# Page numbers read four or six at a time, ahead of the wait for the buffer

## The reference

```python
rows_c = pool_cmp[page_table].reshape(b, past_len, N_KV_HEADS, 2, HEAD_DIM)
o_c, imp = cmp_branch(q, compress(rows_c, w_cmp), q_pos, rel_bias, k_gain[0])
...
_, idx = lax.top_k(score, n_top)
phys = page_table[jnp.arange(b)[:, None, None, None], start // page]
rows = pool[phys[..., None], off, gi]
return sel_attend(q, rmsnorm(rows[..., 0, :], k_gain), rows[..., 1, :], k_pos, q_pos, rel_bias)
```

## Time and profile before

| | us |
|---|---|
| median of 3 runs | 1231.87 (1231.04 to 1232.95) |
| the profiled execution | 1229.76 |
| its span, first to last instruction | 1227.5 |
| PE busy | 1179.2 (96%) |
| DVE, ACT, POOL busy | 477.9, 286.2, 221.9 |

### The profile page before, as it was taken

The page is one execution under the profiler, slowest core; times in us unless marked ns, Lnnn a source line. Parts: engine busy times, 40 slices in busy tenths (PEclk is TensorE's granted clock), DMA queues, the critical chain, the costliest instruction groups (busy, mean ns, idle before and its releaser), DMA issues.

```text
span 1227.5 us, 36608 instructions
## 1 busy us (share of the span) xinstructions
PE 1179.2 (96%) x14724; PEld 971.6 (79%) x14724; DVE 477.9 (39%) x1383; ACT 286.2 (23%) x763; POOL 221.9 (18%) x376
## 2 busy tenths in 40 slices
PE   9999999999999999999878789999999999999998
PEld 7888877999999987874445457797897887977977
DVE  3111115677775333105687763441121221212214
ACT  1000003100010122335978850211011011010022
POOL 5133232011340000413445530100000000000000
PEclk9999999999999999999999999999999999999999
DMA  9998889999442474653687789599999999999821
GB/s 331 328 311 289 296 286 315 182 353 334 144 166 95 180 291 167 165 104 107 205 289 247 249 262 366 200 387 364 381 356 374 366 362 388 336 349 390 297 98 39
DMA packets 123099, 329.99 MB, mean 269 GB/s; under 512 B 17880, under 2 KB 56873, under 8 KB 121268
## 3 DMA queue, kind: packets, MB, share of 16 engines
q1 hardware_dynamic: 96772, 259.88, 58.3%
q0 software_dynamic: 16656, 59.30, 16.6%
q10 hardware_dynamic: 9504, 8.48, 2.3%
HBM read 319.16 MB, written 15.70 MB: 273 GB/s over the span
## 4 chain that ended last, share of the span: by engine, by line
PE 82%; issue 6%; DMA 3%; SPq 3%; POOLq 2%; POOL 2%; ACT 1%; DVE 1%; DVEq 0%; ACTq 0%
PE bank L2097 16%; PE bank L2798 16%; PE bank L2218 12%; PE pbank L2809 6%; PE bank L2254 6%; PE pbank L2798 3%; PE bank L2809 3%; PE bank L2155 3%; PE bank L2343 2%; POOLq L632 2%; SPq L632 1%; PE bank L2750 1%; SPq L642 1%; POOL gring L657 1%; PE bank L2432 1%
## 5 line engine op out<-in xcount | busy, mean ns | idle before, releaser
L2798 PE MATMUL bank<-X,gring 128*64 128x96 f32 x4608 | 196.7, 246 | 5.6 <-issue 5.4
L2798 PEld LDWEIGHTS bank<-X,gring 128*64 128x64 f32 x4608 | 192.3, 137 | 10.5 <-issue 10.5
L2097 PE MATMUL bank<-aT,gring 128*128 128x288 f32 x704 | 175.3, 407 | 2.2 <-DMA gring<-in_conv_in 2.2
L2097 PEld LDWEIGHTS bank<-aT,gring 128*128 128x128 f32 x704 | 133.0, 190 | 39.6 <-DMA gring<-in_conv_in 3.1
L2809 PE MATMUL pbank<-Q,X 128*32 128x256 f32 x1152 | 75.9, 379 | 0.0
L642 POOL DMA_DIRECT2D Q<-in_cache_cmp x96 | 51.9, 541 | 120.1 <-issue 120.1
L2218 PE MATMUL bank<-aT,gring 128*128 128x144 f32 x528 | 72.3, 286 | 0.8 <-issue 0.7
L2023 DVE TENSOR_TENSOR X<-X,bank 128x96 f32<-128x96 f32 x72 | 18.4, 256 | 134.7 <-ACT X L1347 134.2
L2016 DVE TENSOR_TENSOR hT<-hT,bank 128x288 f32<-128x288 f32 x48 | 18.9, 449 | 128.6 <-PE bank L2750 128.6
L2218 PEld LDWEIGHTS bank<-aT,gring 128*128 128x128 f32 x528 | 67.8, 190 | 1.1 <-issue 0.8
L1347 ACT ACTIVATE X<-bank 128x96 f32<-128x96 f32 x72 | 18.2, 253 | 200.6 <-PE bank L2798 200.6
(11 more groups left out here) (409 smaller groups left out, 1819.1 us busy)
## 6 DMA issues: line engine op xcount, KB each, us to landing
gring<-in_moe SPq DMA_DIRECT2D x176, 512.0 KB, 5.9
Q<-in_moe SPq DMA_DIRECT2D x72, 512.0 KB, 7.3
gring<-in_dense_gu SPq DMA_DIRECT2D x44, 512.0 KB, 14.1
gring<-in_conv_in SPq DMA_DIRECT2D x24, 512.0 KB, 8.0
Q<-in_cache_cmp POOLq DMA_DIRECT2D x96, 128.0 KB, 4.0
Q<-in_cache_cmp SPq DMA_DIRECT2D x96, 128.0 KB, 4.0
gring<-in_dense_down SPq DMA_DIRECT2D x16, 704.0 KB, 5.3
Q<-in_cache_cmp ACTq DMA_DIRECT2D x64, 128.0 KB, 3.8
```

What stands on the lines that cost most here:

```text
L2097: ins = pe.matmul(bank(label, k)[:, 0:T], tile[:, 128 * i:128 * i + 128], rhs[:, i, :], start=i == 0, stop=i == C - 1)
L2798: ins = pe.matmul(m_bank(i, M_GU + f)[64 * w:64 * w + 64, CAP * u:CAP * u + CAP], gslot(("m", 0), 2 * f + u)[:, o:o + 64], ae[:, c, :], st ...
```

## The change

Instead of one load per page, ahead of each page's DMA, one instruction reads all page numbers of the tile into registers: four in `four_pages`, six or four in `half_pages`. It and the checks stand ahead of the wait for the buffer. The DMAs, their order, their queues and their waits stay.

```diff
-        def page(eng, b, i):
-
-            return eng.value_load(ptab[0:1, b * PAGES + i:b * PAGES + i + 1], min_val=0, max_val=POOL - 1)
+        def pages_of(eng, b, first, n):
+
+            row = ptab[0:1, b * PAGES + first:b * PAGES + first + n]
+            return nc.values_load_multi_w_load_instructions(row, (eng.engine,), min_val=0, max_val=POOL - 1)[1]
 
         def half_pages(eng, u, h, which, arrived):
 
             k = HALVES_OF[u % 3][h]
+            numbers = pages_of(eng, 2 * (u // 2) + h, which.start, which.stop - which.start)
             if u >= 1 and not (u == 1 and k == 2):
                 full(eng, ("cu", u - 2 if h == EARLY[u % 3] else u - 1))
-            for i in range(which.start, which.stop):
-                src = A["cache_cmp"][bass.ds(page(eng, 2 * (u // 2) + h, i), 1), :, 256 * (u % 2):256 * (u % 2) + 256].rearrange("a p n -> (a p) n")
+            for i, number in enumerate(numbers, which.start):
+                src = A["cache_cmp"][bass.ds(number, 1), :, 256 * (u % 2):256 * (u % 2) + 256].rearrange("a p n -> (a p) n")
...
             n = GN[label]
+            numbers = pages_of(eng, 2 * p + b2, 4 * t, 4)
             g_released(eng, list(GN)[n - GS])
-            for i in range(4):
-                src = A["cache_sel" + kind[1]][bass.ds(page(eng, 2 * p + b2, 4 * t + i), 1), :, :].rearrange("a p n -> (a p) n")
+            for i, number in enumerate(numbers):
+                src = A["cache_sel" + kind[1]][bass.ds(number, 1), :, :].rearrange("a p n -> (a p) n")
```

## The result

The changed kernel took 1220.36 us in the median of 4 runs (1218.09 to 1221.08), the kernel before 1232.41 beside it (4 runs, 1231.04 to 1234.4): ratio 0.9898, 95% interval [0.9879, 0.9917], 12 us less where 8.0 had been forecast. The profiled executions are 1229.76 and 1220.25 us (spans 1227.5 and 1218.5), so the two traces have 9.5 of the 12 us to explain.

A forecast was written before the change was run, and what follows sets the result against it. PE was taken to wait on the issue queues, SP's in the convolution and POOL's in the selected branch. Gains of 2.8 + 5.2 = 8.0 us gave 1231.87 - 8.0 = 1223.9 us, range for 8 in 10 from 1220.2 to 1229.8.

The forecast's parts named there:

- The queues of issue set the pace, in both stages: SP's issue queue in the convolution and POOL's in the selected branch set the pace; forecast case, chance 0.60, 1220.5 to 1226.
- Load of four at 0.288, lower end: One load of four registers costs 0.288 us, range up to 1.15, saving 0.95 us per tile on POOL.
- each register costs a load: Rival: a load of four costs 1.15 us, so only what lies ahead of a wait is gained; 1225.5 us, chance 0.18.
- Checks moved in front of the wait are free: Checks cost nothing where a queue waits anyway; where the wait has ended, the first page leaves about 0.7 us later.
- Convolution 2.8 us: Convolution gain: waits of 2.2 for `conv_in` weights and 1.2 ahead of a `compress`, less 0.6 for traffic.
- The last `compress`: Convolution: its 1.2 us wait goes; its late half was said to have no linears left to cover it.
- Weights issued 4.9 us earlier: Convolution, SP's queue: twelve pages take 8.4 us in place of 13.3, so the weight tile behind them is issued earlier.
- Selected branch 5.2 us: Selected branch gain: 5.7 us of waits for value and key tiles over three pairs, less 0.5 for later landing.
- Pairs at 38.5 to 39 us: Sign in the selected branch: distance between the same value tile of two pairs, in place of 40.4 us.
- POOL's queue alone as the bound there: Selected branch: a pair takes POOL 40.6 us of issue against 40.4 per pair, so POOL's queue sets the pace.
- DMA-bound: Rival: the DMA engines are the bound, earlier issue only lengthens landing; gain perhaps 1.5 us, 1230.4, chance 0.15.
- Slower, a load over 1.24 us: Rival on POOL's queue in the selected branch: a load of four costs more than four loads; around 1238 us, chance 0.05.

The follow-up runs named there:

- light: Changed kernel without the check of each number and with loads of eight from column 0 or 4 in the convolution, ahead of the wait: 1222.74 us, ratio 0.9933.
- merged_behind: Changed kernel with the merged loads and their checks behind the wait for the buffer in both stages: 1233.49 us, ratio 1.0007 to the kernel before.
- behind_sel: Changed kernel with load and checks moved behind the wait in the selected branch (`four_pages`) alone: 1220.49 us, ratio 0.9882 to the kernel before.
- conv_only: Changed kernel with single loads kept in `four_pages`, so new loads in the convolution alone: 1227.59 us, ratio 0.9957 to the kernel before.
- four_two: Changed kernel with the six numbers of a half loaded as four and two: 1223.62 us, ratio 0.9914 to the kernel before.
- sel_only: Changed kernel with single loads kept in `half_pages`, so new loads in the selected branch alone: 1225.80 us, ratio 0.9959 to the kernel before.
- after_again: The changed kernel, unaltered, measured and profiled a second time: 1222.71 us, ratio 0.9893 to the kernel before.

## Why the prediction was right and where it was wrong

The mechanism was right, the size was not. The step that failed is a term of the sum: the convolution was put at 2.8 us and gave 4.7, because a wait of 1.3 us that hangs on the same queue was left out and 0.6 us were taken off for traffic. The selected branch was right in size, 5.2 put and 5.3 measured. On the prediction's own scale the gain was 12.6 us, 4.6 more than forecast. The traces have only 1.5 of these 4.6; the other 3 are the difference between profiled and timed executions, and what caused it stays open.

- *The queues of issue set the pace, in both stages: right.* Each half of the change removes the waits of its own stage, and doubling the new cost in the selected branch brings its waits back, PE's larger than before (5.0 us for 4.2).
- *Load of four at 0.288, lower end: right for the selected branch* (0.328 on POOL, tile 3.66 for 3.6 forecast, queue count x48). *For the six of the convolution it was wrong:* 0.72 and 1.40 us. I took one price for four and six. POOL's six come near the dearer bound, each register a load (6 x 0.288 = 1.73). The rival "each register costs a load" nearly held there, and it cost nothing that the runs show: with 0.57 us instead of 1.40 (`light`) the convolution takes 130.58, as after. The load stood ahead of a wait. The Trainium skill's 200 ns for each register (page "Runtime: NRT & Kernel Launch", section "Instruction fetch mechanics") agrees with the rows where a load goes number by number (0.18 to 0.22 us for each further one), and not with aligned fours (0.02 to 0.04 for three more).
- *Checks moved in front of the wait are free: right for after, and underrated.* I charged the move only where a wait had already ended. `merged_behind` shows that in the convolution the merge without it is worth less than nothing: 2.4 us between release and first page cost more than denser pages bring. In the selected branch `behind_sel` shows that it is hardly needed.
- *Convolution 2.8 us: too small, 4.7 measured.* Two terms failed. The `conv_out` wait of 1.3 us stood in the same view and was left out of the 3.4; it hangs on the same queue. And the 0.6 taken off for traffic was not needed: in 50 to 190 us the DMA engines moved 317 GB/s where they moved 301, and `conv_only` and `four_two` have no wait of PE left there. With both the sum would have been 3.4 + 1.3 = 4.7. That it meets the measured 4.7 to the tenth is partly luck: the trace of after kept 1.0 us of waits and got 0.5 from the overlaps of PE's pieces.
- *The last `compress`: right in the gain, wrong in the reason.* Linears did stand ahead of it to cover its pages, 48 matmuls from 170.70 to 182.60. The wait came because POOL issued its last page only at 177.80; that page landed at 183.72, and `compress` began at 183.81.
- *Weights issued 4.9 us earlier:* SP's twelve pages took 8.9 us for 8.4 forecast, 4.4 us less than the 13.3 of before; enough. SP in order of time after:

```profile
72.04 8.89 SPq L644 DMA_DIRECT2D Q<-in_cache_cmp  x12
```

- *Selected branch 5.2 us: right in size,* 5.3 in the traces of after, `sel_only`, `four_two` and `light`, 2.8 in `after_again`; the times of `sel_only` give 0.9959, 5.1 us. *Pairs at 38.5 to 39 us:* 39.1, nearly.
- *POOL's queue alone as the bound there: wrong.* "What is late next" was asked for ACT's keys in the third pair and not for SP: its `ple_proj` tile had 1.0 us of cover, less than the gain. Had the change been made on POOL alone, my sum for the stage, 5.2, would have met 0.7 us (ratio 0.9994).
- *DMA-bound: fallen.* Median times from issue to landing did grow (`cache_cmp` on POOL from 4.0 to 5.6 us, `selv` from 3.3 to 3.7), as that rival said, but with 0.5 us of waits for pages in their place in the convolution and none in the selected branch: the pages were issued earlier by more than they landed later. *Slower, a load over 1.24 us: fallen* for the fours (0.328). For six the same sum gives 6 x 0.288 + 5 x 0.03 = 1.88, and the 1.40 measured is under it too.
- *Sum.* 4.7 + 5.3 = 10.0, less about 0.25 lost between the stages and 0.75 behind 745 us, is the 9.0 between the spans. The other 2.5 us of the 12 is not located: the profiled execution of before lay some 2.6 under the median beside after, and `after_again` (0.9893) stands by the larger figure. I carried the 2.1 us between profile and median over unchanged; it was no part of the kernel after (1220.25 profiled, 1220.36 median). The low end of the range was also added up wrongly: the waits taken off the full gains are 0.6 + 0.5 = 1.1 us, not 1.3, and even 8.0 + 1.3 + 1.7 leads to 1220.9 and not 1220.2.

## What to carry to other kernels

Where a queue waits for a buffer and then issues indirect loads, count the time from release to the first transfer, not only the length of the burst: address numbers and their checks belong in front of the wait; behind it they can undo what merging saves, as they did where the DMA engines had little room. Read every wait line that hangs on the queue, whatever tensor it names, and ask of each queue that carries the change which later tile stands behind it and with what cover. Start a load of several registers at a multiple of four numbers, and round its size up to a multiple of four.

## What the runs showed of the hardware

- A load of registers from SBUF is cheap by fours only if it begins at a multiple of four: one number 0.27 to 0.31 us, four aligned 0.30 to 0.33, four from column 2 0.97 on POOL, eight aligned 0.53 (SP) and 0.58 (POOL), six from column 6 1.40.
- Denser bursts in a stage at 0.91 of DMA busy still raised what it moved, from 301 to 317 GB/s (50 to 190 us), while the median page of it took 1.0 to 1.6 us longer to land: here a longer time to land was no sign that the engines were the bound.
- The same kernel's profiled spans differed by 5.6 us (1218.5, 1224.1), 2.6 of them in the selected branch, where the granted clock fell at other places. An effect below that can't be read from one trace's span, and one below some 2.6 us not from the distance between two numbered matmuls either; it needs the wait lines of several traces, or timed runs.
